# PEER routing in a fused decoder layer: key scores issued by alternating row halves, and the side work of the routing handed out by elements passed

## What is computed

```python
q = (hf @ wq).reshape(t, PEER_HEADS, 2, PEER_DKEY // 2)           # 8 heads, 2 halves of 64
scores = jnp.einsum("thcd,hcnd->thcn", q, keys)                   # 128 keys for each head and half
s_top, i_top = lax.top_k(scores, PEER_TOPK)                       # 16 of 128
cand = s_top[:, :, 0, :, None] + s_top[:, :, 1, None, :]
best, pos = lax.top_k(cand.reshape(t, PEER_HEADS, 256), PEER_TOPK)
gates = jax.nn.softmax(best, axis=-1)                             # and eidx, the expert of each of the 16
act = jax.nn.gelu(jnp.einsum("thkd,td->thk", u_tab[eidx], xb))
out = jnp.einsum("thk,thkd->td", gates * act, v_tab[eidx])        # 16384 experts of width 1024
```

## Time and profile before

| | |
|---|---|
| median of 3 runs | 1656.91 us (1653.51 to 1660.56) |
| the profiled execution | 1651.35 us |
| its span | 1649.6 us |
| mean granted TensorE clock | 0.963 |
| PE busy | 1563.1 us, 95% of the span |
| DVE busy | 1195.3 us, 72% |
| ACT, POOL busy | 679.9 us, 379.4 us |
| moved by DMA | 403.01 MB, mean 244 GB/s |

### The profile page before, as it was taken

The page is one execution under the profiler, slowest core; times in us unless marked ns, Lnnn a source line. Parts: engine busy times, 40 slices in busy tenths (PEclk is TensorE's granted clock), DMA queues, the critical chain, the costliest instruction groups (busy, mean ns, idle before and its releaser), DMA issues.

```text
span 1649.6 us, 23516 instructions
## 1 busy us (share of the span) xinstructions
PE 1563.1 (95%) x7989; PEld 1351.4 (82%) x7989; DVE 1195.3 (72%) x2146; ACT 679.9 (41%) x1054; POOL 379.4 (23%) x362
## 2 busy tenths in 40 slices
PE   7999989767999999999999999889999999999998
PEld 4877647533989999999999999888888888888886
DVE  3502543547699789989899988449787878888885
ACT  2102444412333577348744586233333333333331
POOL 5533101001611122112111114115322222222210
PEclk9899789788999899999999999999999999999999
DMA  5220213001977688877787788979999999999993
GB/s 218 64 90 15 101 41 126 1 1 44 335 218 242 210 298 309 291 230 271 295 311 243 242 311 325 339 252 377 360 354 320 352 338 345 346 365 351 354 353 138
DMA packets 170145, 403.01 MB, mean 244 GB/s; under 512 B 14176, under 2 KB 96096, under 8 KB 168032
## 3 DMA queue, kind: packets, MB, share of 16 engines
q1 hardware_dynamic: 133216, 268.01, 46.1%
q0 software_dynamic: 36864, 134.23, 23.2%
HBM read 347.67 MB, written 54.53 MB: 244 GB/s over the span
## 4 chain that ended last, share of the span: by engine, by line
PE 79%; DVE 12%; DMA 3%; ACT 3%; issue 2%; SPq 1%; POOL 0%; DVEq 0%; ACTq 0%
PE psum L502 47%; PE psum L1026 32%; DVE ulo L1678 2%; DVE urow L1684 1%; DMA uraw<-in_uT 1%; DMA urow<-in_u,eidx 1%; DVE sco L1760 1%; DVE itop L1764 1%; DVE itop L1758 1%; DMA xT<-in_xT 1%; DVE top L1756 1%; DVE top L1762 0%; ACT pr L1139 0%; DMA aring<-acts_scratch 0%; DVE nk L1616 0%
## 5 line engine op out<-in xcount | busy, mean ns | idle before, releaser
L502 PE MATMUL psum<-hhi,uhi 128*128 128x384 f32 x1024 | 351.1, 343 | 7.2 <-ACT act_s L1340 7.2
L502 PE MATMUL psum<-hlo,uhi 128*128 128x384 f32 x1024 | 346.2, 338 | 0.0
L480 POOL DMA_INDIRECT urow<-in_u,eidx x128 | 151.1, 1181 | 555.0 <-DVE urow L1684 482.2
L1418 ACT ACTIVATE vhi<-vraw 128x1024 fp32r<-128x1024 f32 x128 | 135.9, 1061 | 324.5 <-PE psum L1026 324.5
L1026 PE MATMUL psum<-vhi,wlo 128*128 128x512 f32 x768 | 236.6, 389 | 0.0
L1026 PE MATMUL psum<-vhi,whi 128*128 128x512 f32 x768 | 236.5, 389 | 0.0
L1026 PE MATMUL psum<-vlo,whi 128*128 128x512 f32 x768 | 236.4, 389 | 0.0
L480 POOL DMA_INDIRECT urow<-in_v,eidx x120 | 132.0, 1100 | 382.2 <-DVE acc L1914 381.6
L502 PE MATMUL psum<-hhi,ulo 128*128 128x384 f32 x1024 | 201.0, 337 | 13.0 <-DVE ulo L1678 13.0
L1908 DVE TENSOR_TENSOR vlo<-vraw,vhi 128x1024 fp32r<-128x1024 f32 x128 | 156.7, 1224 | 70.7 <-ACT vhi L1418 70.6
L502 PEld LDWEIGHTS psum<-hhi,uhi 128*128 128x128 f32 x1024 | 195.4, 191 | 8.4 <-ACT uhi L1333 7.8
(11 more groups left out here) (296 smaller groups left out, 2030.0 us busy)
## 6 DMA issues: line engine op xcount, KB each, us to landing
uraw<-in_uT SPq DMA_DIRECT2D x128, 512.0 KB, 5.2
vraw<-in_v SPq DMA_DIRECT2D x128, 512.0 KB, 5.9
acts_scratch<-act_s SPq DMA_DIRECT2D x128, 192.0 KB, 3.7
gates_scratch<-stage SPq DMA_DIRECT2D x12, 2048.0 KB, 9.2
gring<-gates_scratch SPq DMA_DIRECT2D x32, 768.0 KB, 8.6
aring<-acts_scratch SPq DMA_DIRECT2D x128, 192.0 KB, 6.0
wring<-in_chunks SPq DMA_DIRECT2D x23, 512.0 KB, 4.0
wout<-in_wout SPq DMA_DIRECT2D x1, 4096.0 KB, 12.6
```

Of the source, the lines that this page charges most:

```text
L480: g.indirect_dma_start(urow[k], None, table, bass.IndirectOffsetOnAxis(eidx[:, n % HK:n % HK + 1], 0)).then_inc(row_in[k], 16)
L502: return nc.tensor.matmul(out, lhsT, rhs, start=start, stop=stop)
L1418: a_(vhi[:, k, :], vraw[:, k, :], ACT.Copy).then_inc(s["vhi_ready"], 1)
```

## The change

`key_scores` goes through the heads and issues both halves of a head in turn, without the wait between halves; half c of heads 0 to 3 goes to bank 4 + 2c and of heads 4 to 7 to bank 5 + 2c, so that no bank gets both halves. ACT copies the banks in that order with new addresses, and `route` waits for two copies before its first and two more before its third round. Ticks get weights (`TICK_WORK`, roughly the elements that the step before them passes): 4 or 5 for a wide operation, 3 or 4 for a narrow one, 9 or 10 for one on 2048 elements, 195 in all, and blocks, dots and `SOFT_AT` (12 + 1 in place of 13 + 1 blocks after the route's start) follow their sum.

```diff
--- before.py
+++ after.py
@@ -81,7 +81,9 @@
 HOT_AT = [20, 56, 92]
 REST_AT = 108
 EARLY_DOTS = 16
-TICKS = 44
+WIDE, NARROW = [4, 5, 5, 4, 5], [3, 4, 4, 3, 4]
+TICK_WORK = 4 * WIDE + [6] + NARROW + [0] + NARROW + [0, 3, 2, 9, 9, 10, 2, 10, 9, 9]
+TICKS = len(TICK_WORK)
 PAIR_AT = [sum(TOPK // (b + 1) for b in range(a)) for a in range(TOPK)]
 PAIRS = PAIR_AT[-1] + 1
 SOFT_TICK = 33
@@ -91,8 +93,12 @@
 CHUNKS_G = TD // CHUNK_T
 
 
+def share(count, tick):
+    return count * sum(TICK_WORK[:tick]) // sum(TICK_WORK)
+
+
 def lowered_at(t, tick):
-    return ROUTE_AT[t] + ROUTE_U * min(tick, TICKS) // TICKS
+    return ROUTE_AT[t] + share(ROUTE_U, tick)
 
 
 SOFT_AT = [lowered_at(t, SOFT_TICK) + 1 for t in range(NT)]
@@ -919,16 +925,13 @@
                 pe.wait_ge(s["sco_ready"], 4 * t)
                 if t > 1:
                     pe.wait_ge(s["g_free"], 16 * (t - 2) + 2)
-                for c in range(2):
-                    r_ = slice(HD * c, HD * (c + 1))
-                    for i in range(PH // 2):
-                        for h in (2 * i, 2 * i + 1):
-                            a = (2 * (h % 2) + c) * P
-                            last = mm(psum[:, 4 + i, a:a + P], pqT[r_, h, (t - 1) * P:t * P], keysT[r_, h, :])
-                        if c:
+                for h in range(PH):
+                    for c in range(2):
+                        r_ = slice(HD * c, HD * (c + 1))
+                        last = mm(psum[:, 4 + 2 * c + h // 4, (h % 4) * P:(h % 4 + 1) * P],
+                                  pqT[r_, h, (t - 1) * P:t * P], keysT[r_, h, :])
+                        if h % 4 == 3:
                             last.then_inc(s["sco_full"], 1)
-                    if c == 0:
-                        other_rows(last)
 
             def up(k, i):
 
@@ -1317,7 +1320,8 @@
                 act.wait_ge(s["sco_full"], n + 1)
 
                 act.wait_ge(s["routed_ready"], t)
-                a_(sco[:, 2 * i:2 * i + 2, :, :], psum[:, 4 + i, :].rearrange("p (h c n) -> p h c n", h=2, c=2),
+                half, c = divmod(i, 2)
+                a_(sco[:, 4 * half:4 * half + 4, c, :], psum[:, 4 + 2 * c + half, :].rearrange("p (h n) -> p h n", h=4),
                    ACT.Copy).then_inc(s["sco_ready"], 1)
 
             def softmax(t):
@@ -1749,7 +1753,7 @@
                 if t == 0:
                     beside_route0(at[0])
                 else:
-                    up_to(lowered_at(t, at[0]), begun[0] + ROUTE_DOTS * min(at[0], TICKS) // TICKS)
+                    up_to(lowered_at(t, at[0]), begun[0] + share(ROUTE_DOTS, at[0]))
 
             def top16(t, pairs):
 
@@ -1767,7 +1771,7 @@
             def route(t):
                 at[0], begun[0] = 0, dotted[0]
                 for i in range(PH // 2):
-                    dve.wait_ge(s["sco_ready"], 4 * t + i + 1)
+                    dve.wait_ge(s["sco_ready"], 4 * t + (2 * (i // 2) + 2 if t else i + 1))
                     top16(t, [(sco[:, h, c, :], top[:, h, c, :], itop[:, h, c, :]) for h in (2 * i, 2 * i + 1) for c in range(2)])
                     link(v.tensor_copy(itopf[:, 2 * i:2 * i + 2], itop[:, 2 * i:2 * i + 2]))
                 first, second = top[:, :, 0, :], top[:, :, 1, :]
```

## The result

| | before | after |
|---|---|---|
| median of 6 runs | 1653.31 us (1649.57 to 1660.56) | 1630.60 us (1628.56 to 1632.48, and one of 1966.03) |
| ratio, without the run of 1966.03, with 95% interval | | 0.9855 [0.9829, 0.9881] |
| profiled execution, its span | 1651.35, 1649.6 us | 1631.71, 1630.0 us |
| mean granted TensorE clock | 0.963 | 0.969 |

By the ratio the kernel is 1.45% faster, 24.0 us; by the medians in the table it is 22.7 us. The execution of 1966.03 us ran in a slower state, at a mean clock of 0.74: the median of six takes it in, the ratio does not, and without it the median is 1629.48.

A forecast was written before the change was run, and what follows sets the result against it. PE was taken to bound the kernel (busy 95%), losing time to DVE in the first pass. Terms 3.75 + 6.5 + 4.2 + 0.3 + 2.0 = 16.8 us took 1656.9 to 1640.1 us; range 1634 to 1652.

The forecast's parts named there:

- Part 1: End of route 3: block 88 is lowered 3.45 us earlier, so its wait and low clock go; gain 3.75 us, bounds 0 to 3.75.
- Part 2: Route 1, block 15: one wait of some 3 us becomes four shorter ones, the clock fall goes; gain 6.5 us.
- The rival that the falls are this execution's own: Timed runs may have their clock falls elsewhere, so 8.2 us are not there to gain; 1648 to 1651 us, chance 0.10.
- Part 3: Key scores: row halves overlap, 2.0 us a call for 4.1; gain 4.2 us at t = 2 and 3, 0.3 at t = 1.
- the slower rival: Key scores: each change of row half costs a restart, 3 us more a call; 5 us slower, 1662 us, chance 0.05.
- the one without overlap: Key scores: row halves do not overlap, each call gains 0.2 us in place of 2.1; 1644 us, chance 0.13.
- Part 4: Tail after route 3: three gathers and dots fewer; gain 2.0 us, bounds 0 and 4.3 + 2.2.
- The sign "three fewer gathers in 1010 to 1050": Tail of the first pass: three fewer gathers between 1010 and 1050 us would show the forecast right.
- What was late next: Route ends: each route ends 2.3 us later in DVE's time, just covered; at route 3 PE arrives about 0.5 us behind it.
- The collision rival: At 1034 to 1048 us DMA sets the date and hides all earlier gains; 1652 us or more, no change, chance 0.07.
- the chances of faster: Whole kernel: faster by over 0.5% (under 1648.6 us) given 0.72, from forecast, no overlap and three quarters of the third case.

The follow-up runs named there:

- the key scores alone: The kernel before with only the key scores changed (halves in turns, own banks, their copies and waits), ticks as before: 1639.59 us, 0.9924.
- the ticks alone: The kernel before with only the weighted ticks, key scores as before: 1637.8 us, 0.9908.
- the kernel with the old shares of dots: The changed kernel with dots beside the routes given out as before, so three more are left behind route 3: 1639.97 us, 0.9922.
- all five kernels made from it: Kernel before with one dot more a route, 1644.65 us; three gathers cut early, 1654.37, or later, 1650.04; three dots cut, 1650.56, or moved last, 1644.95.

## Why the prediction was right up to the tail, and wrong there

- **Part 1, block 88: right.** 3.75 us forecast; between the transposes after routes 2 and 3 the change gained 14.6 - 10.9 = 3.7. The wait stays with the key scores alone and goes with the ticks alone.
- **Part 2, block 15: the size right, the cause only half.** The four waits at blocks 12 to 15 were forecast as 0.4, 0.5, 0.7 and 1.5 us; the starts of the matmuls in the trace give 0.26, 0.31, 0.57 and 1.47, and no fall. But the change of the wait's shape was not needed: with the key scores alone a wait of 2.84 had no fall behind it. I had ordered the falls by the wait's length alone (1.31 without, 1.88 and 2.85 with); besides the 2.84 without one, 2.42 at 518.23 us had one in the kernel with the old shares of dots.
- **The rival that the falls are this execution's own: refuted.** The kernel before and all five kernels made from it with old routes and old key scores show the same two falls, of 13.7 us beginning 79.1 to 79.2 us behind the first key scores and of 3.4 us at route 3's end.
- **Part 3, key scores: right, and partly luck.** 2.0 us forecast by the pace of the column halves, 2.06 measured; no row had shown that row halves keep that pace. In the trace the two halves of a head start 7 ns apart and the next head 0.105 us later. The Trainium skill, TensorE: Matmul & The Clock Gate, Part 3, taken evenly, would have given 2.7 us; the measurement decides, and it is twice the pace, not the estimate's 1.5 times. The Trainium skill, TensorEngine Tiling (Array Packing), Key Properties, has a change of tile drain nothing: the trace agrees, with 7 ns, so the slower rival is refuted, and so is the one without overlap. The wait at block 0 grew to 2.52 us as forecast; a fall of 3.4 us follows it. Route 1 gains 8.8 us where 8.9 were forecast, so the fall cost nothing visible.
- **Part 4, the tail: this step failed, by the size of its term.** "Bounds 0 and 4.3 + 2.2 ...; I take 2.0, as about half of the missing gathers fall before the collision." Measured: 6.0 (idle 7.2 to 2.3, busy 73.8 to 72.7), near the upper bound. I had asked what share of three average gathers falls before the collision. But the three that go are not average ones: with 19 dots for 16 blocks the loop gives two dots to each of the first three blocks, just ahead of the loads that PE waits for, and with 16 it gives one to each, so that the burst is gone altogether. With the same 19 and the three moved to the end the tail is 72.6 us. The loop is in the code, and POOL's rows with 0.30 us between gathers were in the trace before. The sign "three fewer gathers in 1010 to 1050" is met only near the last gates (six for nine in the stretch of the table); in the whole stretch, which now lies 12.7 us earlier, nine are issued for ten.
- **Not in the sum at all:** the passage to the second pass, where PE waits for block 124 to be lowered: 4.30 us before, 3.05 after. With what follows it makes 1.9 us, of which the second pass gives back 1.1. I had not read these rows; that the change causes this is not shown.
- **What was late next: right.** Route 3 now ends 0.6 us ahead of PE (forecast 0.5), with no wait there. The collision rival, by which all would be hidden, is refuted: the last gates' store and the v loads came 14.6 us earlier too, counted from the first key scores, and the waits there got shorter.

The range failed by 3.4 us. Its lower end allowed for the tail's whole 6.5 us, which by the sum gives 1656.9 - 21.3 = 1635.6 and not 1634, but took the median of three runs, 3.6 above that of six, as fixed, and nothing for the second pass. Two smaller slips bear on nothing: the slower rival's 3.75 / 45 is 0.083, and the chances of faster add up to 0.73.

## What to carry to other kernels

Where a resource is short in one known stretch, read the order in which its other users are issued just ahead of it, not only their number: moving three dots, and with them the gathers that they release, from the front of a loop to its end was worth 8 us here, a third of what the large change brought. A rounding rule that hands out the surplus first (`ceil`) makes a burst at exactly the loop's start. Read every trace of an unchanged stretch for its scatter before taking a difference of one or two microseconds for an effect. And undo each half of a change alone before crediting one with a shared term: 6.5 us of low clock went with either.

## What the runs showed of the hardware

- Two matmuls of 64 rows on the two row halves of the array, fp32, issued in turns and into different banks, run fully beside each other: 32 in 2.06 us in place of 4.15. Order, banks and the wait in the middle were changed together; which of them is needed, no run tells.
- A wait's length did not tell whether the clock falls behind it: 2.84 us without a fall in one place, 2.86 with a fall of 3.4 us, 2.85 with one of 13.7; 2.42 in route 1 and 1.88 in route 3 with one of 3.4; about 2.5 behind the first key scores with one of 3.4 in every kernel with fast key scores; 1.30 at block 15 without one, in the change and with the ticks alone.
- 1.38 MB of gathers fewer changed nothing at one place (81.4 against 81.0 us of tail) and went with 3.6 us less some 20 us later, in the same queue; the total moved by 2.3 us by ratio, with an interval that includes 1. A load of 512 KB, issued in the same order, took 8.5 us until its use with two gathers about it, 15.0 to 17.4 with nine.
- Three dots and the gathers that they release, moved from the first three to the last three of 16 blocks, shortened the tail from 81.0 to 72.6 us, while the lowering of the fourth and fifth block and the start of the v loads kept their times to 0.1 us.
